# Five chains of a streaming encoder step are led through their PSUM banks

## What is computed

```python
proj = x @ w_in                                   # q, k, v and the GLU pair u
q = _partial_rotary(q, pos); k = _partial_rotary(k, pos)
attn = window attention over 64-token chunks, with sinks
c_in = u[..., :CONV_WIDTH] * jax.nn.sigmoid(u[..., CONV_WIDTH:])
c = jax.nn.silu(_layer_norm(_causal_dwconv(c_ext, conv_dw_w, conv_dw_b), conv_ln_g, conv_ln_b))   # 31 taps
mix = jnp.concatenate([attn, c], axis=-1) @ w_out
h = _layer_norm(DEEPNORM_ALPHA * x + mix, ln1_g, ln1_b)
up = h @ w_up
upc = _causal_dwconv(up_ext, ffn_dw_w, ffn_dw_b)                                                   # 3 taps
f = (jax.nn.silu(upc[..., :D_FF]) * upc[..., D_FF:]) @ w_down
ple = jax.nn.sigmoid(h @ w_pg + b_pg) * (p @ w_pe)
y = _layer_norm(DEEPNORM_ALPHA * h + f + ple, ln2_g, ln2_b)
```

## Time and profile before

| | |
|---|---|
| median of 3 runs | 2635.33 us (2635.21 to 2638.05) |
| profiled execution: its time, its span | 2635.92 us, 2634.1 us |
| mean granted TensorE clock | 0.957 of 2.4 GHz |
| PE busy | 2392.4 us (91%) |
| DVE busy | 1920.2 us (73%) |
| POOL busy | 1520.8 us (58%) |
| ACT busy | 1273.8 us (48%) |
| DMA | 341.51 MB, mean 130 GB/s |

### The profile page before, as it was taken

One profiled execution on the slowest core, in us unless ns is written; L12 is line 12 of the kernel. 1 busy time (PEld: TensorE's weight loads), 2 busy tenths in 40 slices (PEclk: granted clock), 3 DMA queues, 4 the chain that ended last, 5 costly groups with the idle time before them and its releaser, 6 DMA issues. The chain is left out here.

```text
span 2634.1 us, 38062 instructions
## 1 busy us (share of the span) xinstructions
PE 2392.4 (91%) x15013; PEld 2347.7 (89%) x15013; DVE 1920.2 (73%) x2367; ACT 1273.8 (48%) x2060; POOL 1520.8 (58%) x648
## 2 busy tenths in 40 slices
PE   7577878989999998999998999999899999968996
PEld 7467878979899998999998999999899999968995
DVE  5846998477888747888765888976689787566843
ACT  4235544455543535554353564545455445445553
POOL 7244566666455466555556645556565554746763
PEclk9788999989999999999999999999999999989998
DMA  6123344544333263333335333334443333524442
GB/s 231 55 95 107 118 145 138 166 134 140 113 120 127 93 194 112 136 117 119 129 112 176 127 118 112 122 121 148 133 160 106 118 125 102 175 89 152 160 145 92
DMA packets 119042, 341.51 MB, mean 130 GB/s; under 512 B 15312, under 2 KB 43600, under 8 KB 118864
## 3 DMA queue, kind: packets, MB, share of 16 engines
q1 hardware_dynamic: 93360, 308.70, 34.7%
q10 hardware_dynamic: 25504, 30.37, 3.5%
HBM read 330.12 MB, written 8.99 MB: 129 GB/s over the span
## 5 line engine op out<-in xcount | busy, mean ns | idle before, releaser
L432 POOL TENSOR_TENSOR w_lo<-w_raw,w_hi 128x1024 fp32r<-128x1024 f32 (+1 forms) x636 | 1519.8, 2399 | 1075.6 <-ACT w_hi L574 1074.7
L574 ACT CAST w_hi<-w_raw 128x1024 fp32r<-128x1024 f32 (+1 forms) x636 | 622.5, 982 | 593.1 <-PE ps L482 461.0
L480 PE MATMUL ps<-h_hi,w_hi 128*128 128x386 f32 (+5 forms) x2496 | 820.4, 329 | 27.2 <-POOL w_lo L432 22.0
L481 PE MATMUL ps<-h_lo,w_hi 128*128 128x386 f32 (+5 forms) x2496 | 810.5, 325 | 0.0
L482 PE MATMUL ps<-h_hi,w_lo 128*128 128x386 f32 (+5 forms) x2496 | 810.4, 325 | 0.0
L480 PEld LDWEIGHTS ps<-h_hi,w_hi 128*128 128x128 f32 x2496 | 477.1, 191 | 36.2 <-POOL w_lo L432 23.8
L481 PEld LDWEIGHTS ps<-h_lo,w_hi 128*128 128x128 f32 x2496 | 477.7, 191 | 1.8 <-issue 0.6
L482 PEld LDWEIGHTS ps<-h_hi,w_lo 128*128 128x128 f32 x2496 | 477.5, 191 | 0.0
L480 PE MATMUL ps<-f_hi,w_hi 128*128 128x384 f32 (+2 forms) x1264 | 419.0, 332 | 30.6 <-POOL w_lo L432 29.0
L481 PE MATMUL ps<-f_lo,w_hi 128*128 128x384 f32 (+2 forms) x1264 | 411.6, 326 | 0.0
L482 PE MATMUL ps<-f_hi,w_lo 128*128 128x384 f32 (+2 forms) x1264 | 410.9, 325 | 0.0
(11 more groups left out here) (119 smaller groups left out, 2397.9 us busy)
## 6 DMA issues: line engine op xcount, KB each, us to landing
w_raw<-in_panels SPq DMA_DIRECT2D x540, 512.0 KB, 3.2
w_raw<-in_panels SPq DMA_DIRECT2D x48, 384.0 KB, 3.1
w_raw<-in_panels SPq DMA_DIRECT2D x48, 128.0 KB, 2.3
xres<-in_xT ACTq DMA_DIRECT2D x32, 192.0 KB, 2.8
out_yT<-res ACTq DMA_DIRECT2D x4, 1536.0 KB, 5.6
a_raw<-in_xT ACTq DMA_DIRECT2D x6, 768.0 KB, 6.5
out_yT<-res ACTq DMA_DIRECT2D x2, 1024.0 KB, 4.6
x_raw<-in_xT ACTq DMA_DIRECT2D x1, 1536.0 KB, 12.0
```

Source lines behind the costliest of these rows:

```text
L432: pool.tensor_tensor(w_lo[:, n % WS, 0:w], w_raw[:, n % RS, 0:w], w_hi[:, n % WS, 0:w].bitcast(F32), ALU.subtract).then_inc(w_lo_done, 1)
L480: pe.matmul(out, w_hi[:, sl, c], hi, start=k == 0, stop=False)
L481: pe.matmul(out, w_hi[:, sl, c], lo, start=False, stop=False)
L574: act.copy(w_hi[:, n % WS, 0:w], w_raw[:, n % RS, 0:w]).then_inc(w_hi_done, 1)
```

## The change

- Silu writes its result into the PSUM bank of the odd u group instead of back into `u_out`. That bank still holds the raw matmul result, so silu now waits until the taps of both halves are done. The product reads and writes that bank, with the value half from `u_out` as its only SBUF input. `f_hi` is made from the bank, and `f_lo` reads the bank and `f_hi`. The bank of an odd u group is given back to PE only after `f_lo`, no longer after the taps.
- The rotary step multiplies by the cosine in place in the group's bank, then adds the bank and the turned product. The cosine product now waits for the shuffle, which reads the same bank. The bank is given back after the sum, no longer after the cosine product.
- The gated embedding multiplies in place in the pe group's bank and adds the bank to `res`. That bank is held for one instruction more; the SBUF gate buffer is free one instruction earlier.
- The root of LayerNorm is written back into its own PSUM bank; the reciprocal works in place there, and the scaling reads it from there. `std` in SBUF is gone. What waited for the root before using that bank now waits for the scaling.

```diff
--- before.py
+++ after.py
@@ -287,7 +287,6 @@
     prob_t = place("prob_t", [N_HEADS, P], offset=sq_base + N_HEADS * P * 4)
     v_tok = place("v_tok", [6, P], offset=sq_base + 2 * N_HEADS * P * 4)
     assert (2 * N_HEADS + 6) * P <= KB * WM
-    std = place("std", [WM])
     par = place("par", [PARAM_COLS])
     u_state = place("u_state", [2 * FB, FHALO])
     u_last = place("u_last", [2, 2 * FB, FHALO])
@@ -321,8 +320,7 @@
     table_in = [sem("table_in0"), sem("table_in1")]
     xres_in = [sem(f"xres_in{k}") for k in range(XS)]
     p_in, p_hi, p_lo = sem("p_in"), sem("p_hi"), sem("p_lo")
-    gate_done, glu_done, qk_read, qk_done, v_done = (
-        sem(n) for n in ("gate_done", "glu_done", "qk_read", "qk_done", "v_done"))
+    gate_done, glu_done, qk_done, v_done = (sem(n) for n in ("gate_done", "glu_done", "qk_done", "v_done"))
     conv_in, conv_read, halo_done = sem("conv_in"), sem("conv_read"), sem("halo_done")
     z_done, down_done, sig_done, ple_done, ple_added = (
         sem(n) for n in ("z_done", "down_done", "sig_done", "ple_done", "ple_added"))
@@ -356,17 +354,20 @@
         elif kind == "in" and k == IN_V:
             eng.wait_ge(v_done, t + 1)
         elif kind == "in":
-            eng.wait_ge(qk_read, t * (1 + HB) + (k - IN_V if k >= IN_Q else 0) + 1)
+            eng.wait_ge(qk_done, t * (1 + HB) + (k - IN_V if k >= IN_Q else 0) + 1)
         elif kind == "out":
             eng.wait_ge(z_done, t * KB + k + 1)
         elif kind == "u":
-            eng.wait_ge(taps_done, t * 2 * FB + k + 1)
+            if k % 2:
+                eng.wait_ge(f_lo_done, t * FB + k // 2 + 1)
+            else:
+                eng.wait_ge(taps_done, t * 2 * FB + k + 1)
         elif kind == "d":
             eng.wait_ge(down_done, (t * 3 + k) * KB + e[3] + 1)
         elif kind == "pg":
             eng.wait_ge(sig_done, t * KB + k + 1)
         else:
-            eng.wait_ge(ple_done, t * KB + k + 1)
+            eng.wait_ge(ple_added, t * KB + k + 1)
 
     def prompt_and_sample(t, prompt_at, sample_at):
 
@@ -491,7 +492,7 @@
                     pe.wait_ge(const_set, 1)
                 else:
                     before = LN_NO["ln2", t - 2] if t >= 2 else LN_NO["ln1", 0]
-                    pe.wait_ge(std_done, before + 1)
+                    pe.wait_ge(scaled, before + 1)
                 for n, (c, keys) in enumerate(windows(t)):
                     mm = pe.transpose(ps[0:keys, AUX + n // 4, n % 4 * P:n % 4 * P + P], v_ext[:, t % 2, c:c + keys], ident[:])
                 mm.then_inc(vt_done, 1)
@@ -674,15 +675,15 @@
 
             def silu(t, j):
                 n = t * FB + j
-                act.wait_ge(taps_done, 2 * n + 1)
-                r = u_out[:, n % 2, 0, 0:WIDTH[t]]
-                act.activation(r, r, ACT.Silu).then_inc(silu_done, 1)
+                act.wait_ge(taps_done, 2 * n + 2)
+                act.activation(ps[:, bank(("u", t, 2 * j + 1)), 0:WIDTH[t]], u_out[:, n % 2, 0, 0:WIDTH[t]], ACT.Silu
+                               ).then_inc(silu_done, 1)
 
             def f_high(t, j):
                 n, s = t * FB + j, t * (FB + PB) + j - FS
                 act.wait_ge(prod_done, n + 1)
                 slot_read(s)
-                act.copy(f_hi[:, f_slot(t, j), 0:WIDTH[t]], u_out[:, n % 2, 1, 0:WIDTH[t]]).then_inc(f_hi_done, 1)
+                act.copy(f_hi[:, f_slot(t, j), 0:WIDTH[t]], ps[:, bank(("u", t, 2 * j + 1)), 0:WIDTH[t]]).then_inc(f_hi_done, 1)
 
             def slot_read(s):
 
@@ -712,7 +713,7 @@
                 n = t * KB + m
                 computed(act, e)
                 if n >= 2:
-                    act.wait_ge(ple_added, n - 1)
+                    act.wait_ge(ple_done, n - 1)
                 act.activation(gate[:, n % 2, 0:WIDTH[t]], ps[:, bank(e), 0:WIDTH[t]], ACT.Sigmoid, bias=prm("b_pg", m)
                                ).then_inc(sig_done, 1)
 
@@ -769,9 +770,7 @@
             def root(name, t):
                 n, w = LN_NO[name, t], WIDTH[t]
                 act.wait_ge(var_done, n + 1)
-                if n:
-                    act.wait_ge(scaled, n)
-                act.activation(std[:, 0:w], ps[:, AUX + 1, 0:w], ACT.Sqrt, bias=eps[:, 0:1]).then_inc(std_done, 1)
+                act.activation(ps[:, AUX + 1, 0:w], ps[:, AUX + 1, 0:w], ACT.Sqrt, bias=eps[:, 0:1]).then_inc(std_done, 1)
 
             def affine(name, t):
                 z, hi, lo, nb, w = ln_of(name, t)
@@ -895,15 +894,12 @@
                     computed(dve, e)
                     tmp = turned[:, n % 2, 0:w]
                     own.step(dve.stream_shuffle(tmp, src[:, 0:w], SHUFFLE))
-                    for tok, cnt, dst in parts:
-                        ins = dve.tensor_tensor(dst, src[:, tok:tok + cnt], cos[:, t % 2, tok:tok + cnt], ALU.mult)
-                    ins.then_inc(qk_read, 1)
                     own.wait()
+                    own.step(dve.tensor_tensor(src[:, 0:w], src[:, 0:w], cos[:, t % 2, 0:w], ALU.mult))
                     own.step(dve.tensor_tensor(tmp, tmp, sin[:, t % 2, 0:w], ALU.mult))
                     own.wait()
-                    dve.wait_ge(qk_read, n + 1)
                     for tok, cnt, dst in parts:
-                        ins = dve.tensor_tensor(dst, dst, tmp[:, tok:tok + cnt], ALU.add)
+                        ins = dve.tensor_tensor(dst, src[:, tok:tok + cnt], tmp[:, tok:tok + cnt], ALU.add)
                     ins.then_inc(qk_done, 1)
 
             def take_out(e):
@@ -933,14 +929,14 @@
                 n, w = t * FB + j, WIDTH[t]
                 dve.wait_ge(silu_done, n + 1)
                 dve.wait_ge(taps_done, 2 * n + 2)
-                dve.tensor_tensor(u_out[:, n % 2, 1, 0:w], u_out[:, n % 2, 0, 0:w], u_out[:, n % 2, 1, 0:w], ALU.mult
-                                  ).then_inc(prod_done, 1)
+                both = ps[:, bank(("u", t, 2 * j + 1)), 0:w]
+                dve.tensor_tensor(both, both, u_out[:, n % 2, 1, 0:w], ALU.mult).then_inc(prod_done, 1)
 
             def f_low(t, j):
                 n, w, s = t * FB + j, WIDTH[t], f_slot(t, j)
                 dve.wait_ge(f_hi_done, n + 1)
-                dve.tensor_tensor(f_lo[:, s, 0:w], u_out[:, n % 2, 1, 0:w], f_hi[:, s, 0:w].bitcast(F32), ALU.subtract
-                                  ).then_inc(f_lo_done, 1)
+                dve.tensor_tensor(f_lo[:, s, 0:w], ps[:, bank(("u", t, 2 * j + 1)), 0:w], f_hi[:, s, 0:w].bitcast(F32),
+                                  ALU.subtract).then_inc(f_lo_done, 1)
 
             def split_p(t):
                 dve.wait_ge(p_hi, t + 1)
@@ -973,13 +969,13 @@
             def take_ple(e):
                 _, t, m = e
                 w, n = WIDTH[t], t * KB + m
-                g, r = gate[:, n % 2, 0:w], res[:, m, 0:w]
+                g, r, both = gate[:, n % 2, 0:w], res[:, m, 0:w], ps[:, bank(e), 0:w]
                 computed(dve, e)
                 dve.wait_ge(sig_done, n + 1)
                 dve.wait_ge(down_done, (t * 3 + 1) * KB + KB)
-                dve.tensor_tensor(g, g, ps[:, bank(e), 0:w], ALU.mult).then_inc(ple_done, 1)
+                dve.tensor_tensor(both, both, g, ALU.mult).then_inc(ple_done, 1)
                 dve.wait_ge(ple_done, n + 1)
-                dve.tensor_tensor(r, r, g, ALU.add).then_inc(ple_added, 1)
+                dve.tensor_tensor(r, r, both, ALU.add).then_inc(ple_added, 1)
 
             marks = []
 
@@ -1069,7 +1065,7 @@
                 z, hi, lo, nb, w = ln_of(name, t)
                 n = LN_NO[name, t]
                 if n:
-                    dve.wait_ge(std_done, n)
+                    dve.wait_ge(scaled, n)
                 if name == "cln":
                     dve.wait_ge(att_done, unit_no(t, UNITS[t]))
                     own.wait()
@@ -1093,10 +1089,11 @@
             def scale(name, t):
                 z, hi, lo, nb, w = ln_of(name, t)
                 dve.wait_ge(std_done, LN_NO[name, t] + 1)
-                own.step(dve.reciprocal(std[:, 0:w], std[:, 0:w]))
+                std = ps[:, AUX + 1, 0:w]
+                own.step(dve.reciprocal(std, std))
                 own.wait()
                 dve.wait_ge(centred, LN_NO[name, t] + 1)
-                dve.tensor_tensor(z, z, std[:, 0:w].unsqueeze(1).broadcast_to([P, nb, w]), ALU.mult).then_inc(scaled, 1)
+                dve.tensor_tensor(z, z, std.unsqueeze(1).broadcast_to([P, nb, w]), ALU.mult).then_inc(scaled, 1)
 
             def rest(name, t):
                 z, hi, lo, nb, w = ln_of(name, t)
```

## The result

The kernel after takes 2571.23 us in the median of 4 runs (2569.08 to 2572.75), the kernel before beside it 2635.46 (4 runs): ratio 0.9748, 95% interval 0.9735 to 0.9762. That is 64 us faster; 75 were forecast (2560), and the range of 2540 to 2597 holds the time. The two profiled spans, 2634.1 and 2570.9 us, are 63.2 us apart.

What follows compares the result with a forecast made beforehand. PE, busy 91%, was taken as the bound, waiting mostly for DVE, late at certain places. Stage gains plus 8 us for the clock summed to 74.8 us, giving 2560 us; 8-in-10 range 2540 to 2597.

Steps and rivals of the forecast that it cites:

- the clock: All stages: with waits removed, half-speed matmuls and pipeline refilling behind them go too; 8 us, between 0 and 14.
- Rival D: LayerNorm's reciprocal in PSUM takes twice as long, 5.1 for 2.54 us, in five chains: 10 us, so 2570; chance 0.06.
- 226 to 330: First tile's divisions: shorter product and `f_lo` ahead of them cut three PE waits of 16.5 us by 8, between 4 and 15.
- 600 to 2280: Four wide tiles: eight division waits and those before the first d groups go, 16 us, between 9 and 17.
- 330 to 401: Stretch bound by DVE: its slot falls under PE's, so the backlog does not form; 18.6 us, between 12 and 18.6.
- 401 to 600: Embedding's pg slots 4.6 us, and 2 of the tree behind the first late product; between 2 and 9.
- The head: 26 to 160, first tile: eight rotary sums shorten from 12.2 to 3.8 us; 8 us gained, between 4 and 11.
- The last tile: 2280 to 2420: shorter products and `f_lo` before the third tree and first d group, and the scaling; 7.2 us, between 3 and 10.
- A: ACT's order and silu's longer wait keep wide-tile waits for division and d groups; gain 40 us, about 2595; chance 0.14.
- B: Product and `f_lo` were stretched only where DVE had time; only the DVE-bound stretch gives, 10 us: 2625; chance 0.05.
- C: Odd group's bank held too long, PE waits at 22 pairs of first and last tile, 66 us: slower, 2660; chance 0.04.
- E: More than the sum: unblocked POOL leaves the trees more room and the clock stays up more often: 2530; chance 0.05.

Runs made afterwards that it cites:

- short subtraction: Kernel before, with POOL subtracting only the first 128 of up to 1024 columns of each weight panel, part of the computation left out: 2483.47 us.
- e3: Kernel before, with the odd bank of each pair given back only after `f_lo`, all operations unchanged: 2638.33 us, ratio 1.0000.
- Early silu: Kernel after, with the value half's last tap writing its own PSUM bank and silu starting after its own half's taps, staying in SBUF: 2566.39 us.

## Why the prediction was right or wrong

**What bounds it, and the mechanism: right.** DVE is late at certain places, through instructions that exclude POOL's. The short subtraction and the 117 stretched products show it directly. The total is partly luck: without the clock the stages came out at -2.8, 0, +1.9, -3.0, -3.1, +4.7, -1.5 and +0.1 us against their forecasts, and these misses partly cancel.

**The price of an operand in PSUM: right.** I took 0.40 to 0.56 us, and for an output in PSUM nothing; `f_lo`, which reads PSUM and writes SBUF, has 414/548/560 ns against 414/550/560 for the same from SBUF. The product, which also writes PSUM, has 432/567/567 against 425/558/561: 6 to 9 ns, where my bound was 500. The Trainium skill's section on the TRN2 errata ("VectorE: DVE Perf Modes") would have `f_lo` 65 ns longer; the two rows differ by 2 ns or less.

**Rival D: dead.** The reciprocal takes 2557 for 2540 ns in the median; 2.5 us more were priced.

**226 to 330, and 600 to 2280: right.** The division's 16.5 us became 8.3, as the 8 forecast. In the wide tiles 16 us of waits were forecast and 20.7 us came; the waits of rows 10 other than L547 went entirely, and by the measure of the next paragraph the rest of the 4.7 is half-speed matmuls and pipeline refilling behind them, which the prediction had put into the clock's 8. L547 stayed (30.1 and 30.7).

**The clock: a size, 8 forecast, under 4 came.** Take for each matmul the time to the next one's start beyond what one takes at full clock. Summed over the stretches at 1.2 GHz, stalls above 0.3 us left aside, this falls from 33.0 to 29.3 us: 3.7. The stalls themselves fall from 238.9 to 180.2, by 58.7 against 66.8 forecast, and 0.9 us comes from matmuls at full clock. So of the nearly 12 us missed, 8 are waits and 4 the clock. The last digit depends on what is taken as full clock. In 330 to 401, the stage from which I had argued the 8, this loss was only 0.5 us before and rose to 1.5: TensorE stood at 1.2 GHz there while it waited anyway.

**330 to 401: "I take all 18.6" was too much, by 3.** The chain of silu, product and `f_lo` now ends after the bank is wanted, once, and PE falls to half clock behind it: a wait of PE for `f_lo`, one of my signs of being wrong. I had costed the hold at nothing, with some 2 us left, and DVE's slot at 5.4 us under PE's 6.0. That margin was not there: DVE's busy time and its wait for silu fill 52.0 us beside PE's 52.3, since my slot left out what DVE does between the slots, such as one sum of 2048 columns that takes 4.0 us. The hold alone costs nothing in the kernel before (e3); in the kernel after it was not tried alone. Early silu, with the same hold, gives 2.1 of the 3 back, 1.5 of them matmuls that no longer run at half clock. DVE idles 90.9 / 132 = 0.69 us before a product; 0.5 to 0.6 was forecast.

**401 to 600: 6.6 forecast, 3.5 came.** The two pg waits fell from 5.8 to 4.6 us only, and those for the trees from 15.2 to 14.5, where I had taken 4.6 and 2. ACT's and DVE's order of time in the kernel after:

```profile
426.86 0.39 ACT L679 ACTIVATE ps<-u_out 128x256 f32<-128x256 f32 x1 [0.73 <-DVE u_out L925]
...
427.27 1.28 ACT L773 ACT_TABLE_LOAD   x1
...
429.14 1.28 ACT L717 ACT_TABLE_LOAD   x1
...
431.10 0.38 ACT L686 CAST f_hi<-ps 128x256 fp32r<-128x256 f32 x1
...
431.51 0.42 DVE L938 TENSOR_TENSOR f_lo<-ps,f_hi 128x256 fp32r<-128x256 f32 x1 [3.79 <-ACT f_hi L686]
```

DVE's instructions are short and it idles 3.79 us: the chain is ACT's, with root and sigmoid and a table load of 1.28 us before each, and it starts later by silu's 0.73 us. Early silu won 1.3 us in this stage. I had read the chain's length from DVE's part of it.

**The head: 8 forecast, 5.2 came, and here the mechanism failed and not only a size.** I took 8.4 us from the rotary sums and nothing back. DVE from 26 to 113, multiplication with sin in the kernel before, then the same and the sum in the kernel after:

```profile
L902 DVE TENSOR_TENSOR turned<-turned,sin 128x256 f32<-128x256 f32 (+1 forms) x10 | 6.7, 674 | 0.0
```

```profile
L899 DVE TENSOR_TENSOR turned<-turned,sin 128x256 f32<-128x256 f32 (+1 forms) x10 | 11.9, 1188 | 0.0
...
L902 DVE TENSOR_TENSOR q<-ps,turned 128x256 f32<-128x256 f32 (+1 forms) x8 | 3.9, 491 | 0.3
```

The sums fell from 12.2 to 3.9 us as forecast, and the two sums for k, which I had left out, from 3.1 to 1.0. But the sin product, which still has two SBUF inputs, rose from 6.7 to 11.9: the collision moved to the neighbouring pair in the chain. With the cosine product's 0.3 us more the ten rotary steps give 4.9 us, close to the 5.2 of the stage. The last tile may be the same on a smaller scale: 7.2 forecast, 5.7 came, with longer trees (146.4 and 151.6 us over all). Whether collisions there moved rather than vanished was not tried.

**The other rivals.** A (ACT as the wall) held at two places, 401 to 600 and silu's wait, for 5 us, not 35. B is out at 64 us. C cost one wait of 1.9 us. E is out: the trees gained nothing.

## What to carry to other kernels

Before giving GpSimd a two-input subtraction, count the VectorE instructions with two SBUF inputs that run beside it: each may be stretched, fourfold here, and one operand in PSUM freed it here at less than 10 ns, where the bank was free long enough. When such a chain has two stretched instructions in a row, moving one to PSUM can hand part of the stretch to the other, as in the rotary step, so cost the chain, not the instruction. Leave the start of the other engine's step where it was: a wait added to it is hidden only where its engine is not next in line, and a wait under a new name is not yet a new cost.

## What the runs showed that I had not expected

- Waiting for a releaser and being blocked by POOL can stand in for each other: with silu late in the kernel before, DVE idled 66 us more before the product, its busy time fell from 1920 to 1860 us, and the median stayed the same.
- POOL is blocked too. Three subtractions beside the stretched tree at 515 took 10.10 us together (3.3, 3.8 and 3.0), where one takes 2.35 in the mean.

```profile
513.45 10.10 POOL L433 TENSOR_TENSOR w_lo<-w_raw,w_hi 128x1024 fp32r<-128x1024 f32 x3 [3.93 <-ACT w_hi L575]
```

- Nearly the same small wait with and without a fall of the clock: in both traces of the kernel after (waits of 1.9 and 1.8 us) TensorE went down to 1.2 GHz for a moment (mean 0.97 in that stretch), in both with early silu (1.5 us) it stayed at 2.4 GHz (1.00). Whether the wait is what brings the fall was not tried.
